# A merged norm, a reordered latent stage and transferred rotations in a five-layer mixer kernel

## The reference

```
def rms_norm(x, gain):
    return x * rsqrt(mean(x * x) + 1e-6) * gain
# every layer of the second block
hx = rmsnorm(x, g_pre[l]) * (1 + scale_x) + shift_x
hc = rmsnorm(ctx, g_pre[l]) * (1 + scale_c) + shift_c
yx, yc = mixer(hx, hc)
x, ctx = x + gate_x * rmsnorm(yx, g_post[l]), ctx + gate_c * rmsnorm(yc, g_post[l])
# layers 0 and 3: q = rmsnorm(cq, g_q) @ w_q, k and v = rmsnorm(ckv, g_kv) @ w_kv; 8 heads of 128 + 64 (rotated)
# layer 1: 16 query heads and 4 key heads of 64, rotated by position; a query block of 128 tokens
# sees the 256 context tokens and its own and the neighbouring blocks; softmax with a sink column
```

## Time and profile before

| | |
|---|---|
| runs | 3205.8 us median of 3 (3202.1 to 3213.0) |
| profiled execution | 3212.75 us, its span 3210.8 us |
| TensorE (PE) busy | 2943.1 us, 92% of the span |
| VectorE (DVE) busy | 1833.1 us, 57% |
| ScalarE (ACT) busy | 1186.3 us, 37% |
| GpSimd (POOL) busy | 93.8 us, 3% |
| mean granted TensorE clock | 0.971 |

### The profile page before, as it was taken

One profiled execution on the slowest core, in us unless ns is written; L12 is line 12 of the kernel. 1 busy time (PEld: TensorE's weight loads), 2 busy tenths in 40 slices (PEclk: granted clock), 3 DMA queues, 4 the chain that ended last, 5 costly groups with the idle time before them and its releaser, 6 DMA issues.

```text
span 3210.8 us, 36048 instructions
## 1 busy us (share of the span) xinstructions
PE 2943.1 (92%) x14454; PEld 2354.4 (73%) x14454; DVE 1833.1 (57%) x3248; ACT 1186.3 (37%) x2079; POOL 93.8 (3%) x176
## 2 busy tenths in 40 slices
PE   7999879999999999999997888999998887989997
PEld 5767648778888788887886666788875556777886
DVE  5445678877676555443635455474535667455544
ACT  4234243232222434444534444452322110454543
POOL 0000000100000100000100000011000000000000
PEclk9999989999999999999999999999999998999999
DMA  6223115645454321002210000233312111322002
GB/s 230 87 85 99 59 53 203 221 151 181 151 189 144 140 92 46 27 1 99 86 52 15 20 7 1 99 107 115 109 52 83 59 47 33 112 86 68 31 1 92
DMA packets 105472, 283.53 MB, mean 88 GB/s; under 512 B 17046, under 2 KB 36535, under 8 KB 105048
## 3 DMA queue, kind: packets, MB, share of 16 engines
q1 hardware_dynamic: 94040, 243.81, 23.0%
q0 software_dynamic: 9392, 32.48, 2.8%
q10 hardware_dynamic: 1872, 4.93, 0.4%
HBM read 257.05 MB, written 24.12 MB: 88 GB/s over the span
## 4 chain that ended last, share of the span: by engine, by line
PE 79%; DVE 11%; ACT 8%; issue 1%; ACTq 0%; DMA 0%; POOL 0%; SPq 0%; DVEq 0%; POOLq 0%
PE ps L1676 19%; PE ps L1678 19%; PE ps L1677 19%; PE ps L1896 4%; PE ps L1709 3%; PE ps L1954 2%; PE ps L1928 2%; PE ps L1883 2%; ACT pt L2229 1%; PE ps L1970 1%; ACT tmp L2221 1%; ACT tmp L2055 1%; PE ps L1809 1%; PE ps L1917 1%; DVE tmp L2572 1%
## 5 line engine op out<-in xcount | busy, mean ns | idle before, releaser
L1676 PE MATMUL ps<-hh,whi 128*128 128x256 f32 (+1 forms) x2424 | 918.3, 379 | 26.9 <-DVE hl L2405 14.4
L1678 PE MATMUL ps<-hh,wlo 128*128 128x256 f32 (+1 forms) x2424 | 871.5, 360 | 0.0
L1677 PE MATMUL ps<-hl,whi 128*128 128x256 f32 (+1 forms) x2424 | 871.3, 359 | 0.0
L1676 PEld LDWEIGHTS ps<-hh,whi 128*128 128x128 f32 x2424 | 459.8, 190 | 134.1 <-issue 27.4
L1677 PEld LDWEIGHTS ps<-hl,whi 128*128 128x128 f32 x2424 | 461.2, 190 | 89.8 <-issue 20.9
L1678 PEld LDWEIGHTS ps<-hh,wlo 128*128 128x128 f32 x2424 | 459.0, 189 | 71.0
L2414 DVE TENSOR_TENSOR wlo<-raw,whi 128x1024 fp32r<-128x1024 f32 x249 | 304.2, 1223 | 243.0 <-ACT whi L2032 242.6
L2032 ACT ACTIVATE whi<-raw 128x1024 fp32r<-128x1024 f32 x249 | 262.7, 1056 | 323.6 <-PE ps L1678 304.2
L1896 PE MATMUL ps<-pt,v 128*128 128x256 f32 x768 | 217.1, 406 | 32.6 <-ACT pt L2229 28.4
L2229 ACT ACTIVATE pt<-ps 128x512 f32<-128x512 f32 (+1 forms) x200 | 109.8, 576 | 200.8 <-PE ps L1883 200.4
L1896 PEld LDWEIGHTS ps<-pt,v 128*128 128x128 f32 x768 | 138.6, 200 | 60.3 <-ACT pt L2229 42.6
(11 more groups left out here) (357 smaller groups left out, 4616.7 us busy)
## 6 DMA issues: line engine op xcount, KB each, us to landing
raw<-in_wall SPq DMA_DIRECT2D x249, 512.0 KB, 4.3
mb<-in_wmod SPq DMA_DIRECT2D x128, 512.0 KB, 3.6
xb<-xpark SPq DMA_DIRECT2D x24, 384.0 KB, 4.7
xpark<-F POOLq DMA_DIRECT2D x32, 256.0 KB, 2.3
upark<-tmp POOLq DMA_DIRECT2D x18, 384.0 KB, 2.7
u<-upark SPq DMA_DIRECT2D x24, 256.0 KB, 3.1
early<-in_wm SPq DMA_DIRECT2D x8, 512.0 KB, 6.2
early<-in_wmod POOLq DMA_DIRECT2D x8, 512.0 KB, 7.1
```

What stands on the lines that cost most here:

```text
L1676: e.matmul(out, L[0], R[0], start=start, stop=False)
L1677: e.matmul(out, L[0], R[1], start=False, stop=False)
L1678: return e.matmul(out, L[1], R[0], start=False, stop=stop)
```

## The change

- **Between the blocks.** The context's squares, sums, root and norm for layer 0 (`context_norm`) are staged between the eight output tiles of the feed-forward's second half, which no longer pump. The squares of `x` are added up on VectorE, once weighted by `gain^2 + 1e-6` and once plain (`square_add`). After the last tile two matmuls (`gain_sum`) give the sum for both norms at once, with 1e-12 as constant; `first_in` issues the context's products of three tiles, then two matmuls of the plain sum, eight matmuls of zeros, and the products of `x`. `x` is scaled by the first norm (`final`) later, between tiles 4, 5 and the key tile, and parked from there. The setup of layer 1 moves to layer 1.
- **Latents.** Squares right behind tile 3, sums behind tile 4; squares of 4 and 5 behind tile 5, sums behind the key tile; in layers 0 and 3.
- **Matmuls of zeros**: those ahead of the sums of the norm 2, of the latents of layers 0 and 3 and of the first score of layer 1 go (14, 12, 12 and 17), and the 22 of layer 0 become 8.
- **Rotations**, in all three attention layers: one ScalarE copy to SBUF, four transfers on SyncE's queue that swap quarters, three VectorE operations. `rope_add` goes behind the next unit, `stack` or `rope_split` behind the one after. In layer 1 the query tiles with odd number keep both behind the next unit, and the context's `stack` is put off too.
- **Layer 1**: units of up to 512 keys use one bank of each pair, by turns; `make_v` claims banks 5 to 7; `make_k` moves from behind unit 5 to behind unit 4.

```diff
-    idle_before = {2: 14, ("lat", 0, 0): 12, ("lat", 3, 0): 12, "out": 9, "head": 10, "tile": 17}
+    idle_before = {"out": 9, "head": 10}
...
+        def turn():
             stage("rope_add", c_ - a_, cs, j, m, name)
             tmps.drop(j)
+        def halves():
             stage("rope_split", m, c_ - a_, hi, lo, name, free)
             tmps.drop(m)
-        later(rest)
+        later(turn)
+        later(halves, 1)
...
+    def context_norm(c):
+        if c < 4:
+            if c == 0:
+                for key in ("sh0", "sc0"):
+                    need(key)
+                stage("coef_in", 0)
+                stage("coef_gain")
+                entry["b"] = [banks.take()]
+            t = [tmps.take() for _ in range(2)]
+            for i in range(2):
+                stage("square", (10, 0), F, [(s_ctx, "ctx")], 2 * c + i, 0, NC_, t[i])
+            def after():
+                for i in range(2):
+                    stage("sum_squares", (10, 0), 2 * c + i, KD, CSEG, entry["b"], t[i])
+                    tmps.drop(t[i])
+                if c == 3:
+                    entry["R"] = tmps.take()
+                    stage("rstd", [((10, 0), 0, NC_, D, CSEG, entry["b"], entry["R"], (pe, ("sq", (10, 0), KD - 1)))])
+                    banks.drop(*entry["b"])
+            return after
+        for k in (2 * c - 8, 2 * c - 7):
+            t = tmps.take()
+            stage("norm_a", (10, 0), k, [(s_ctx, "ctx")], CSEG, (COEF[:, 40:48],), (MODC[:, 48:56],), (dve, ("coef_in", 0)), 0, entry["R"],
+                  (act, ("rstd", (10, 0))), (pe, last_tile["gates"]), t)
+            stage("norm_b", (10, 0), k, CSEG, (MODC[:, 48:56],), 0, t, *([entry["R"]] if k == KD - 1 else []))
+            tmps.drop(t)
+        if c == 7:
+            tmps.drop(entry["R"])
+        return lambda: None
+    def square_sums(c):
...
+        stage("square", 2, F, [(dve, ("ffn", 1, c))], c, NC_, T, t)
+        if c < KD - 1:
+            stage("square_add", c, entry["sums"], t)
+            tmps.drop(t)
+        else:
+            entry["last"] = t
...
+                if half:
+                    square_sums(c)
             return evac
         for c in range(8):
-            play(tile_stages(11, HB, hsrc, XSEG, ev_ffn(c), off=NC_))
+            after = context_norm(c) if half else None
+            play(tile_stages(11, HB, hsrc, XSEG, ev_ffn(c), off=NC_, pumps=1 - half))
+            if after:
+                after()
         align()
-    xf = [[(dve, ("ffn", 1, c))] for c in range(8)]
-    R = rms_stages(2, F, xf, NC_, T, D, KD)
...
+    def first_in(evac):
+        sums, t = entry["sums"], entry["last"]
+        bk = [[banks.take()] for _ in range(2)]
+        stage("gain_sum", bk[0][0], sums[0], t)
+        R = tmps.take()
+        stage("rstd", [((10, NC_), NC_, T, D, XSEG, bk[0], R, (pe, "gain_sum"))])
+        banks.drop(*bk[0])
         for k in range(KD):
-            for a, b in SEGS:
-                stage("park", l, k, a, b, tx[k])
-        R = rms_stages(10 + l, F, tx, 0, T, D, KD)
-        h_done[l] = dict.fromkeys((0, NC_), (dve, ("H", 10 + l, KD - 1)))
-        return norm_stages(10 + l, tx, SEGS, (COEF[:, c + 8:c + 16], COEF[:, c:c + 8]),
-                           (MODC[:, c0:c0 + 8], MODX[:, c0:c0 + 8]), (dve, ("coef_in", l)), 0, R, (act, ("rstd", 10 + l)), hfree)
+            stage("park", 0, k, 0, NC_, [(s_ctx, "ctx")])
+        sx, sc, both = normed(0)
+        first = Two(3, 3, KD, H, sc, sx, True, CSEG, XSEG)
+        for n, (i, k) in enumerate(first.steps):
+            first.main(i, k)
+            if n == 8:
+                stage("plain_sum", bk[1][0], sums[1], t)
+                tmps.drop(*sums, t)
+        prev = None
+        for k in range(KD):
+            t = tmps.take()
+            stage("norm_a", (10, NC_), k, [(dve, ("ffn", 1, k))], XSEG, (COEF[:, 32:40],), (MODX[:, 48:56],), (dve, "coef_gain"), 0, R,
+                  (act, ("rstd", (10, NC_))), (pe, last_tile["gates"]), t)
+            if prev:
+                stage("norm_b", (10, NC_), prev[0], XSEG, (MODX[:, 48:56],), 0, prev[1])
+                tmps.drop(prev[1])
+            prev = (k, t)
+            if k == 4:
+                for i in range(3):
+                    evac(i)(first.main_tiles[i])
+        stage("norm_b", (10, NC_), prev[0], XSEG, (MODX[:, 48:56],), 0, prev[1], R)
+        tmps.drop(prev[1], R)
+        first.ctx_tiles[0].warm = [(None, 8)]
+        for n, (i, k) in enumerate(first.steps):
+            first.context(i, k)
+            if n % KD == KD - 1:
+                ahead(min(wt["at"] // 8 + AHEAD, wt["limit"]))
+        h_done[0] = {a: (dve, ("H", (10, a), KD - 1)) for a in (0, NC_)}
+        for i in range(3):
+            evac(i)(first.ctx_tiles[i])
+        stage("rope2_in")
+        def final():
+            yield
+            R = tmps.take()
+            stage("rstd", [(2, NC_, T, D, XSEG, bk[1], R, (pe, "plain_sum"))])
+            banks.drop(*bk[1])
+            for k in range(KD):
+                if k == 4:
+                    yield
+                stage("final_gain", k, R, [R] if k == KD - 1 else [])
+                stage("park", 0, k, NC_, T, [(dve, ("xf", k))])
+            tmps.drop(R)
+        return both, final()
...
+            self.rests, self.side = deque(), [0, 0]
...
-                self.rests.append(f)
+                while len(self.rests) <= n:
+                    self.rests.append([])
+                self.rests[n].append(f)
...
-                u["bk"].append(tuple(banks.claim(2 * s + i) for i in range(1 if u["w"] == 256 else 2)))
+                if u["w"] > 512:
+                    u["bk"].append((banks.claim(2 * s), banks.claim(2 * s + 1)))
+                else:
+                    u["bk"].append((banks.claim(2 * s + self.side[s]),))
+                    self.side[s] = 1 - self.side[s]
...
-            b, rests = self.before, self.rests or ()
-            self.before, self.rests = u, []
+            b, rests = self.before, self.rests.popleft() if self.rests else ()
+            self.before = u
...
+            def turn():
                 stage("rope_add", NX, CS2, j, m, name)
                 tmps.drop(j)
+            def stack():
                 stage("stack", None, None, TMP[:, m.i, 0:NX], m, dst[:, :, a:b], name, free)
                 tmps.drop(m)
-            later(rest)
+            later(turn)
+            later(stack, 1)
         else:
-            stage("stack", g, bank, ps[:, bank.i, 0:b - a], None, dst[:, :, a:b], name, free)
-            banks.drop(bank)
+            def stack():
+                stage("stack", g, bank, ps[:, bank.i, 0:b - a], None, dst[:, :, a:b], name, free)
+                banks.drop(bank)
+            if context:
+                context(stack)
+            else:
+                stack()
...
-        for c in (4, 5):
-            play(tile_stages(KD, H, tH, SEGS, cq(c)))
+        squares = latent_squares(0, 4, gr)
+        play(tile_stages(KD, H, tH, SEGS, cq(4)))
+        latent_norm(0, 4, gr, 512, col("gq", 4 * j, 4), squares)
+        if done:
+            next(done)
+            next(done)
+        play(tile_stages(KD, H, tH, SEGS, cq(5)))
+        if done:
+            next(done, None)
+        squares = latent_squares(4, 2, SEGS)
         play(tile_stages(KD, H, tH, SEGS, ev_kr))
-        latent_norm(0, 4, gr, 512, col("gq", 4 * j, 4))
+        latent_norm(4, 2, SEGS, 256, col("gkv", 2 * j, 2), squares)
...
-            play(tile_stages(KD, H, tH, None, evac, tok=6))
+            play(tile_stages(KD, H, tH, None, evac, tok=6, at=(5, 6, 7)))
...
-                for i, (a, b) in enumerate(g.groups):
-                    stacked(g, i, Q2[:, q.i, :, :], ("q2" if a == NC_ else "q2c", l, n), (q, free), att.later)
+                for i, (a, b) in reversed(list(enumerate(g.groups))):
+                    later = att.later if n % 2 == 0 else lambda f, n=0: att.later(f)
+                    stacked(g, i, Q2[:, q.i, :, :], ("q2" if a == NC_ else "q2c", l, n), (q, free), later, later)
...
-                              "scale": 0.125, "f0": 256, "w": P * len(keys),
+                              "scale": 0.125, "f0": 256 if len(keys) > 4 else 0, "w": P * len(keys),
...
-                    if qt == 5 and tile % 2 == 0 and tile < 6:
+                    if qt == 4 and tile % 2 == 0 and tile < 6:
...
+        def gain_sum(bk, j, t):
+            w.wait_ge(*dve.of(("sqa", 0, KD - 2)))
+            w.wait_ge(*emptied(bk))
+            e.matmul(ps[:, bk.i, 0:NX], ones[:, :], TMP[:, j.i, NC_:T], start=True, stop=False)
+            w.wait_ge(*act.of(("sq", 2, KD - 1)))
+            w.wait_ge(*dve.of("coef_gain"))
+            e.matmul(ps[:, bk.i, 0:NX], COEF[:, 15:16].broadcast_to([P, P]), TMP[:, t.i, NC_:T], start=False, stop=True).then_inc(*pe.up("gain_sum", j))
...
-                if qt == 2 and h == 0 and s == 0:
-                    warm(bk[0], (None, idle_before["tile"]))
...
-            n = src.shape[1]
-            wait_all(w, (pe, g), j)
```

(77 more changed lines are left out.)

71 lines of the change are left out of this document (32 added, 39 removed).

## The result

The changed kernel takes 3189.9 us (median of 7 executions, 3177.5 to 3192.9) against 3207.8 for the kernel before: ratio 0.9936, interval 0.9919 to 0.9952. That is 18 us less, where 59 were forecast. The profiled execution is the fastest of the seven: span 3175.7 us, clock 0.970 (0.965 to 0.968 in the other six). PE is busy 2901.7 us in it (2943.1 before), still 91% of the span.

A forecast was written before the change was run, and what follows sets the result against it. TensorE, busy for 92% of the span, was taken as the bound, so its idle time and zeros count. Terms summed to -58.5 us: 3212.75 profiled became 3154, less 7 for the median, 3147 us; range 3126 to 3170.

The forecast's parts named there:

- Layer 1's tiles: Layer 1's attention tiles: shorter waits around the query's tail and the key product, -25.6 us in all.
- even tiles: Layer 1's tiles with a key product: the query's tail hides under that product, -7.2 us each, -21.6 for three.
- rival B: Layer 1's gain doesn't come, VectorE's chain stays serial and waits move on; 3168 us, chance 0.14.
- Between the blocks: Feed-forward's end to layer 0's products: 29.4 us without products go, 3.4 of context sums return; net -26.0 us.
- Latents: Latents of layers 0 and 3: zeros and waits ahead of the sums go, -10.7 us.
- Late modulations and rotations at the first scores: First scores of layers 0 and 3: modulation rows done late cost +7 us, rotations by transfers +2.6.
- Rival D: Late modulations and rotations hide and the fuller TensorE holds its clock; 3126 us, chance 0.13.
- the heads: Layer 0's heads: eight more late modulation rows, mostly beside products, cost +2 us.
- Layer 1's start: Layer 1's first score no longer waits for value evictions and 17 zeros, -7.8 us.
- Bank alternation: Layer 1's small units taking banks by turns: alone brings nearly nothing, since scores were ready when VectorE came.
- Rival C: Without the zeros the clock falls, 1.7 us at each of six places, 10 us; 3157 us, chance 0.08.
- Rival E: Slower: rotation transfers wait on SyncE's queue with weight tiles behind them; 20 sets, 120 us, 3267 us, chance 0.03.

The follow-up runs named there:

- ctx_now: The changed kernel with the context half of an odd tile's query in layer 1 stored at once, not one push later; 3152.9 us, ratio 0.9815.
- ctx_k5: ctx_now with layer 1's key product one push later, behind unit 5 as in the kernel before; 3170.0 us, ratio 0.9872.
- ctx_mods: ctx_now with one modulation transfer and its VectorE sums back in each output tile of the feed-forward's second half; 3159.1 us, ratio 0.9837.
- ctx_rope: ctx_now with small scores always in their pair's first bank, plus the old rotation (four ScalarE copies, no transfers) in all three attention layers; 3149.5 us, ratio 0.9812.
- ctx_zeros: ctx_now with the 17 matmuls of zeros put back ahead of layer 1's first score; 3160.1 us, ratio 0.9840.
- k_late: The changed kernel with layer 1's key product behind unit 5, as in the kernel before, late context store kept; 3184.3 us, ratio 0.9908.
- fixed_banks: The changed kernel with scores of at most 512 columns always in their pair's first bank, late context store kept; 3176.8 us, ratio 0.9897.

## Why the prediction was wrong

The direction was right and the time was 43 us off, outside the range. The step that failed is in "Layer 1's tiles", even tiles: "the whole tail of the query falls under `make_k`'s 8 x 1.04 = 8.3 us of products". It was walked on VectorE's queue alone. The products can't begin until the tail is over, since the tail's last store empties the bank that they claim. So 21.6 us of gain met 3 x 7.69 = 23.1 us of wait: -2.2 and +4.7 us where -25.6 stood. ctx_now takes only the late store away and has tiles of 47.0 and 41.0 us and 3152.9 in all, inside the forecast's own range. The place of the key product was right (17 us, ctx_k5); putting off the context's store, which the sum counted only as a part of 2.9 us on VectorE's queue, was the part that cost. Of rival B, the gain's absence was right, and its reason (a serial VectorE chain) was wrong.

Not all of the 43 us is this step. In the second profile (3185.9 us) the gain falls some 32 short: 30.3 in the tiles, 5.6 in layer 2, 0.8 in the other rows, less 4.9 of a faster start. The forecast had also taken 7 us off for the median of three executions against the profiled one, and the median of seven lies 4 us above this profile.

- Between the blocks: -26.0 against -25.5. That the modulations have to leave the feed-forward for this gain was not seen (ctx_mods). In the working, half of the clock's 3.7 us is 1.9, not 1.7, which changes nothing.
- Latents: -10.7 against -11.4 and -11.5.
- Late modulations and rotations at the first scores: +9.6 against +8.7 and +9.0, of which ctx_rope gives 1.7 and 1.8 to the rotations (2.6 in all were taken). Rival D, that they hide, falls. In the heads the total, +2 against +3.5 and +2.9, was near, but not its making: ctx_mods puts 7.2 on the eight rows, so some 4 us seem to have been gained there by what the prediction had not named. No run tells by what.
- Layer 1's start: -7.8 against -7.1; the zeros put back delay the score by 3.7.
- Bank alternation "brings nearly nothing": right that it takes no wait away in sum, wrong that it is free. It costs 8 to 9 us by the medians.
- Rival C: nothing shows that the places without zeros pay. Between the blocks the clock is 1.00 where the window with 36 zeros had 0.94, and the one place where a run put zeros back, layer 1's, became slower (ctx_zeros). What lowers the clock in layer 1 stays open. The Trainium skill, "TensorE: Matmul & The Clock Gate", on oscillation in real kernels, ties the low clock to idle gaps; the traces agree only in part: 0.92 and 0.95 in layer 1 with three waits of 7.69 us and 0.96 without them, but 0.95 in the kernel before and 0.91 in k_late, which don't have them either (their longest are 3.6 and 4.6 us).
- Rival E falls: VectorE waits for a transfer four times in the whole changed kernel, 11.2 us in all, twice of them beside the value tile of layer 1, so they show in TensorE's time only at the first scores of layers 0 and 3. With ScalarE's copies in their place layer 1's tiles are 8.3 us longer.

## What to carry over

A store that is deferred keeps its source buffer. Before deferring an eviction, list who claims that bank next and whether this product stands before or behind the new place; walking the queue of the engine that does the store doesn't show it. An edit that is right by itself (product earlier: 17 us) can be worth nothing when another (store later) holds the buffer that it needs; a run for each edit, with and without the other, tells them apart. A wait moved from a score to the transpose behind it is no gain. Work that is moved within VectorE's queue costs what stands behind it in its new place: the eight modulation rows cost 7.2 us beside the heads and 12.7 in the feed-forward.

## What the runs showed of the hardware

- Idle time and the granted clock of layer 1's attention don't go together in a simple way. From the changed kernel's profiles to ctx_now's, PE's idle time in the stage falls by 24.4 and 21.8 us and its busy time by 2.0 and 11.6, with the clock going from 0.95 and 0.92 to 0.96. But k_late, with 64 us of idle time and no wait above 4.7 us, has 0.91, and fixed_banks, with 73 us and the three waits of 7.69, has 0.95. The stage in ctx_now, k_late and fixed_banks:
```profile
1635.26:1968.03 332.77, 282.13 (x1567) 235.19 (x1565) 194.11 (x504) 151.83 (x396) 0.00 (x0) 0.96 0.08 23
```
```profile
1642.81:2002.89 360.08, 295.99 (x1566) 247.08 (x1565) 194.50 (x504) 151.78 (x396) 0.00 (x0) 0.91 0.08 21
```
```profile
1638.48:1996.90 358.42, 284.97 (x1566) 234.42 (x1565) 193.81 (x504) 151.02 (x396) 0.00 (x0) 0.95 0.08 21
```
- The same kernel, with the same waits, had 0.95 in that stage in one execution and 0.92 in another, 6.9 us apart. The start up to 1000 us and layer 2, which no edit touches, differ by up to 6.7 and 5.6 us between profiles: one profile against one profile is a poor measure of the whole.
- Seventeen matmuls of zeros ahead of layer 1's attention didn't raise the kernel's mean clock (0.968 to 0.970, against 0.972 to 0.973 without them).
- Four transfers of 64 KB between partitions of SBUF take SyncE 2.41 us to issue, and the median one of 80 lands 2.0 us after its issue:
```profile
1748.87 2.41 SPq L3163 DMA_DIRECT2D tmp<-tmp  x4
```
```profile
tmp<-tmp SPq DMA_DIRECT2D x80, 64.0 KB, 2.0
```
